# Moving five sixths of layer 1's conditioning from the attention into the scan, and keeping the sample states in a ring of six

## The reference

```python
def ada_modulation(c, w, b):
    mod = jax.nn.silu(c) @ w + b
    return jnp.split(mod[:, None, :], 6, axis=-1)
...
def modulate(h, shift, scale):
    return h * (1.0 + scale) + shift
...
    for layer in range(DEPTH):
        mp = ada_modulation(c_prompt, ada_w[layer], ada_b[layer])
        ms = ada_modulation(c_sample, ada_w[layer], ada_b[layer])
```

```python
    states = jnp.einsum('bclgn,bclgrp->bcgrpn', br, xdt * to_end[..., None])
    chunk_decay = jnp.exp(a_cum[:, :, -1])
    def step(h, inp):
        s_c, d_c = inp
        return h * d_c[..., None, None] + s_c, h
...
    y_off = jnp.einsum('bclgn,bcgrpn->bclgrp', cr, h_prev) * jnp.exp(a_cum)[..., None]
    y = (y_diag + y_off).reshape(bsz, length, nh, hp)
```

## Time and profile before

| | |
|---|---|
| median of 3 runs (lowest, highest) | 1770.33 us (1770.12, 1774.13) |
| the profiled execution, its span | 1765.11 us, 1763.3 us |
| TensorE products, weight loads | 1453.4 us (82%), 1060.0 us (60%) |
| VectorE, ScalarE, GpSimd | 651.5 us (37%), 461.8 us (26%), 210.8 us (12%) |
| mean granted clock of TensorE | 0.901 of full |
| moved by DMA | 399.72 MB, 227 GB/s over the span |
| 40 loads of `ada_w` in the attention | 1024 KB each, median 6.3 us from issue to landing |

### The profile page before, as it was taken

How to read it: one execution, slowest core, us unless ns; L and a number is a source line. 1 busy time by engine, 2 the same in 40 slices (tenths; PEclk the granted TensorE clock), 3 DMA queues, 4 the chain that set the end, 5 groups by cost and what they waited for, 6 DMA issues and landing times. The chain is left out here.

```text
span 1763.3 us, 25117 instructions
## 1 busy us (share of the span) xinstructions
PE 1453.4 (82%) x10159; PEld 1060.0 (60%) x10159; DVE 651.5 (37%) x1268; ACT 461.8 (26%) x804; POOL 210.8 (12%) x334
## 2 busy tenths in 40 slices
PE   4999789868879687799579978847999839997883
PEld 1999544446669443499345544437999826554443
DVE  3322266552336466752521111144246361111114
ACT  3212265542224352331301100032224230110012
POOL 0000033210000044100011111040000001111104
PEclk8999899879989788799779999967999969999995
DMA  7222497629932510511789999951232298999984
GB/s 294 72 90 79 184 361 265 246 108 371 364 97 72 201 46 0 203 48 49 314 327 392 384 393 397 398 182 40 81 96 76 72 411 326 385 387 396 398 303 158
DMA packets 133592, 399.72 MB, mean 227 GB/s; under 512 B 15842, under 2 KB 67682, under 8 KB 110690
## 3 DMA queue, kind: packets, MB, share of 16 engines
q1 hardware_dynamic: 114370, 359.01, 54.2%
q10 hardware_dynamic: 11488, 21.24, 3.3%
q0 software_dynamic: 7616, 17.84, 3.2%
HBM read 368.72 MB, written 37.19 MB: 230 GB/s over the span
## 5 line engine op out<-in xcount | busy, mean ns | idle before, releaser
L2889 PE MATMUL ex_gups<-ex_gu,ex_he 128*64 128x256 f32 x1728 | 211.2, 400 | 47.5 <-DMA ex_gu<-in_moe_w_up 44.6
L2889 PEld LDWEIGHTS ex_gups<-ex_gu,ex_he 128*64 128x64 f32 x1728 | 126.6, 143 | 116.0 <-DMA ex_gu<-in_moe_w_up 49.2
L2934 DVE TENSOR_TENSOR ex_hid<-ex_sg,ex_gups 128x128 f32<-128x128 f32 x64 | 18.4, 288 | 298.1 <-ACT ex_sg L2958 298.1
L2907 PE MATMUL ex_yps<-ex_dn,ex_hid_t 128*64 128x512 f32 x512 | 123.9, 604 | 0.9 <-issue 0.9
L2867 POOL DMA_INDIRECT ex_hg<-h_rows,route_tok x64 | 60.2, 941 | 508.4 <-PE ex_trps L2879 424.9
L225 PE MATMUL sc_ps<-h_hi,sc_hi 128*128 128x272 f32 x352 | 101.7, 289 | 0.5 <-PEq L3133 0.5
L225 PE MATMUL sc_ps<-hT_r,sc_hi 128*128 128x272 f32 x352 | 100.9, 287 | 0.0
L225 PE MATMUL sc_ps<-h_hi,sc_w_r 128*128 128x272 f32 x352 | 100.7, 286 | 0.0
L2958 ACT ACTIVATE ex_sg<-ex_gups 128x128 f32<-128x128 f32 x64 | 17.8, 278 | 299.2 <-PE ex_gups L2889 299.2
L2948 ACT ACTIVATE ex_yo<-ex_yps 128x512 f32<-128x512 f32 x64 | 38.3, 598 | 184.8 <-PE ex_yps L2907 184.8
L2927 DVE COPY ex_he<-ex_trps 128x512 f32<-128x512 f32 x64 | 44.3, 692 | 64.7 <-PE ex_trps L2879 64.7
(11 more groups left out here) (539 smaller groups left out, 3369.0 us busy)
## 6 DMA issues: line engine op xcount, KB each, us to landing
ex_dn<-in_moe_w_down SPq DMA_DIRECT2D x64, 1024.0 KB, 26.3
ex_gu<-in_moe_w_gate SPq DMA_DIRECT2D x54, 1024.0 KB, 24.5
ex_gu<-in_moe_w_up SPq DMA_DIRECT2D x54, 1024.0 KB, 26.5
ada_rest_w<-in_ada_w SPq DMA_DIRECT2D x40, 1024.0 KB, 6.3
as_pages<-in_cache_kT SPq DMA_DIRECT2D x32, 512.0 KB, 6.8
as_pages<-in_cache_v SPq DMA_DIRECT2D x32, 512.0 KB, 5.6
y_rows<-ex_yo ACTq DMA_DIRECT2D x128, 128.0 KB, 7.0
qkv_w<-in_mix_w_in SPq DMA_DIRECT2D x12, 1024.0 KB, 5.3
```

The lines of the kernel that those rows point to most:

```text
L2889: last = nc.tensor.matmul(gu_ps[64 * q:64 * q + 64, :, :], he[n % 2][:, j, :], ex.gu[n % S][:, :, j, q * P:(q + 1) * P], start=(j == 0), s ...
L2907: last = nc.tensor.matmul(y_ps[n % 2][64 * c:64 * c + 64, :], hid_t[:, m * CAP:(m + 1) * CAP], ex.dn[n % S][:, m, c * 512:(c + 1) * 512], ...
L2934: nc.vector.tensor_tensor(hid[:, :], sg[:, :], gu_ps[:, 1, :], ALU.mult).then_inc(done["hid"], 1)
```

## The change

- A part is 1024 columns wide. The attention makes five such parts, the last four sixths of layer 0 and the first sixth of layer 1 (20 MB, six slots). Layer 0's first two sixths are still made at the start.
- The other five sixths of layer 1 (20 MB, 40 tiles of 512 KB) are made in the scan, with two slots. Each scan step has three points on TensorE: after the decay sums, after the outputs, and at the step's end. From point 6 on (step 2) each point has one contraction tile; after eight comes a point with the part's turn (two transposes). ScalarE copies the sums, VectorE stores them at the same points, and folds the gains in step 17.
- The sample states live in a ring of six. States 6 and 7 are loaded in step 13, after states 0 and 1 have been updated and stored. Their sums are made in step 14 (before 10) and turned in step 16 (before 12); the third pair's turn stays in step 12.
- SyncE's list is written by points: the late tiles' loads, the stores of the states (each now after its own update, no longer behind the last chunk state), the wait for the first two stores.
- Chunk 3 is prepared in steps 8 to 11 (before 9 to 12).
- The conditioning takes a PSUM bank. To free it, the sums made at the start share a bank with the outputs, and the product of B and C goes into the second half of the turning bank: the next turn waits until VectorE has masked it.
- The wait for the last states' stores is also put at ScalarE's end in the next stage.

```diff
 class AdaWeights:
-    COLS = 2048
-
-    def __init__(self, k, name, parts, slots, ctx, at=None):
-        self.k, self.parts, self.slots = k, parts, slots
-        if at is None:
+    def __init__(self, k, name, parts, slots, ctx, at=None, cols=2048, rows_at=None):
+        self.k, self.parts, self.slots, self.COLS = k, parts, slots, cols
+        if rows_at is not None:
...
     def turn(self, turn_ps):
-        for c in range(4):
+        for c in range(self.COLS // 512):
...
     PREPARE = {0: [(1, 0)], 1: [(1, 1)], 2: [(1, 2)], 3: [(1, 3)],
-               4: [(2, 0)], 5: [(2, 1), (4, 0)], 6: [(2, 2), (4, 1)], 7: [(2, 3), (4, 2), (4, 3)],
-               9: [(3, 0)], 10: [(3, 1)], 11: [(3, 2)], 12: [(3, 3)]}
-    SUMS_AT, TURN_SUMS_AT = {9: (0, 1), 10: (2, 3)}, {11: (0, 1), 12: (2, 3)}
+               4: [(2, 0)], 5: [(2, 1), (4, 0)], 6: [(4, 1), (2, 2)], 7: [(2, 3), (4, 2), (4, 3)],
+               8: [(3, 0)], 9: [(3, 1)], 10: [(3, 2)], 11: [(3, 3)]}
+    SUMS_AT, TURN_SUMS_AT = {9: (0, 1), 10: (2,), 14: (3,)}, {11: (0, 1), 12: (2,), 16: (3,)}
     FIRST_UPDATE = 11
+    RING = 6
+    LATE_PARTS, LATE_SPAN, LATE_FROM = 5, KT + 1, 6
+    late_products, late_turn, late_copy = {}, {}, {}
+    for part in range(LATE_PARTS):
+        base = LATE_FROM + LATE_SPAN * part
+        for j in range(KT):
+            late_products[base + j] = (part, j)
+        late_copy[base + KT - 1], late_turn[base + KT] = part, part
...
-        sst = k.sb("sst", [P, NB, D], ctx=ctx)
-        ac_ps = k.ps("ss_acps", [P, 512], ctx)
+        sst_ring = k.sb("sst", [P, RING, D], ctx=ctx)
+        ada = AdaWeights(k, "ada_late", [(1, part) for part in range(1, 1 + LATE_PARTS)], 2, ctx, cols=1024,
+                         rows_at=k.offset["neg_ones"])
...
+        ac_ps = y_ps[1]
+        ada_bank = k.ps("ss_ada", [P, 512], ctx)
+        ada_ps = ada_bank[:, 0:256]
...
+                def load_late(m):
+                    sp.wait_ge(ada.used, m - ada.slots + 1)
+                    ada.load(sp, m // KT, m % KT)
...
+                for point in range(3 * (FIRST_UPDATE + NB)):
+                    part, j = late_products.get(point, (LATE_PARTS, 0))
+                    if part * KT + j + ada.slots < LATE_PARTS * KT:
+                        load_late(part * KT + j + ada.slots)
+                    step = point // 3
+                    if point % 3 == 1:
+                        if step == 17:
+                            sp.wait_ge(s["y"], N)
+                            out_ahead.load(sp)
+                        if step == FIRST_UPDATE + 2:
+                            sp.wait_ge(s["first_out"], 32)
+                            load_states(3)
+                    if point % 3 < 2:
+                        continue
+                    if step == POS[3, 1]:
+                        store_prompt_state()
+                    if step >= FIRST_UPDATE:
+                        store_state(step - FIRST_UPDATE)
...
                     if turn_no[c, part]:
                         pe.wait_ge(s["trc"], turn_no[c, part])
+                    if pairs_before[c, part]:
+                        pe.wait_ge(s["cbc"], pairs_before[c, part])
...
+                def condition(point):
+                    if point in late_products:
+                        part, j = late_products[point]
+                        m = part * KT + j
+                        if j == 0 and part:
+                            pe.wait_ge(ada.out, part)
+                        pe.wait_ge(ada.ready[m % ada.slots], 16 * (m // ada.slots + 1))
+                        ada.products(ada_ps, part, j)
+                    if point in late_turn:
+                        pe.wait_ge(ada.copied, late_turn[point] + 1)
+                        ada.turn(ada_ps)
...
                 for i in range(FIRST_UPDATE + NB):
                     if i < N:
                         decay_sums(i)
+                    condition(3 * i)
                     if 1 <= i <= N:
                         outputs(i - 1)
+                    condition(3 * i + 1)
...
                     if i >= FIRST_UPDATE:
                         update_product(i - FIRST_UPDATE)
+                    condition(3 * i + 2)
...
-                    rest = [(0, 1), (0, 2), (1, 0), (1, 1), (1, 2)]
-                    phase_attention_prompt(k, vtok, mixT, qn, kn, AdaWeights(k, "ada_rest", rest, 3, cw))
+                    rest = [(0, 2), (0, 3), (0, 4), (0, 5), (1, 0)]
+                    phase_attention_prompt(k, vtok, mixT, qn, kn, AdaWeights(k, "ada_rest", rest, 6, cw, cols=1024))
```

More of the change, by code:

```diff
@@ L885, in _ @@
                         dve.wait_ge(ada.turned, store_at[step] + 1)
[L886 removed]
+                        ada.store(ada_ps, store_at[step])
                     if step < STEPS:
@@ L1478, in phase_ssd, with takes @@
             if part < 3:
-                turn_no[c, part] = len(turn_no)
+                turn_no[c, part], pairs_before[c, part] = len(turn_no), pairs
+            if part == 2:
+                pairs += 1
         for t in TURN_SUMS_AT.get(step, ()):
-            turn_no["sums", t] = len(turn_no)
+            turn_no["sums", t], pairs_before["sums", t] = len(turn_no), pairs
     cb_no = {c: i for i, c in enumerate((0, 1, 2, 4, 3))}
[L1484 to L1489, removed]
+    bank_no, uses = {}, [0, 0]
+    def takes(g, *what):
+        bank_no[what] = uses[g]
+        uses[g] += 1
+    for step in range(FIRST_UPDATE + NB):
+        for t in SUMS_AT.get(step, ()):
+            takes(t % 2, "sums", t)
+        for g in range(2):
+            if step < N and UNITS[step][1] == 1:
+                takes(g, "chunk", UNITS[step][0], g)
+            if step >= FIRST_UPDATE:
+                takes(g, "update", step - FIRST_UPDATE, g)
+    names = ("made", "tr", "trc", "dA", "ac_mm", "aexp", "own_d", "xdt", "xw", "cbc", "mat", "mat4", "sums",
              "e", "decx", "m", "cs", "y", "yo", "sload", "stored", "bm", "skip4", "decayed", "oc", "masked", "own_p",
-             "zeroed", "turned", "upper")
+             "zeroed", "turned", "upper", "first_out")
     s = {n: k.sem("ss_" + n) for n in names}
@@ L1551, in _, with load_states @@
             def _(sp):
-                sp.dma_start(sst[:, :, :], io["ssm_state"]).then_inc(s["sload"], 16)
+                def load_states(t):
+                    one = (2 * t) % RING
+                    sp.dma_start(sst_ring[:, one:one + 2, :], io["ssm_state"][:, 2 * t:2 * t + 2, :]).then_inc(s["sload"], 16)
+                for m in range(ada.slots):
+                    ada.load(sp, 0, m)
+                for t in range(RING // 2):
+                    load_states(t)
                 sp.wait_ge(s["zeroed"], 1)
@@ L1556, in _, with store_state @@
                                  zeros[:, :].unsqueeze(1).to_broadcast([P, 4, 256])).then_inc(s["stored"], 16)
[L1557 to L1560, removed]
+                def load_late(m):
+                    sp.wait_ge(ada.used, m - ada.slots + 1)
+                    ada.load(sp, m // KT, m % KT)
+                def store_state(b):
@@ L1561, in _ @@
                     for g in range(2):
[L1562 to L1568 removed]
+                        sp.wait_ge(emptied[g], bank_no["update", b, g] + 1)
@@ new lines, in store_state, with store_prompt_state @@
+                    done = out_ahead.late if b >= NB - out_ahead.KEPT else s["first_out"] if b < 2 else s["stored"]
+                    sp.dma_start(io["ssm_s"][:, b, :], state(b)).then_inc(done, 16)
+                def store_prompt_state():
+                    for g in range(2):
+                        sp.wait_ge(emptied[g], bank_no["chunk", 3, g] + 1)
+                    sp.dma_start(io["ssm_p"], st[:, 1, :]).then_inc(s["stored"], 16)
+                for point in range(3 * (FIRST_UPDATE + NB)):
[14 more added lines that the diff above has]
+                        store_prompt_state()
+                    if step >= FIRST_UPDATE:
+                        store_state(step - FIRST_UPDATE)
```

91 lines of the change are left out of this document (56 added, 35 removed).

## The result

The changed kernel takes 1783.74 us in the median of five runs (1781.48 to 1788.5), the kernel before, run beside it, 1770.33 (1768.8 to 1774.13). The ratio is 1.0079, 95% interval 1.0059 to 1.0099: slower by 0.8%, 13.4 us. The forecast was 1773 with a range of 1757 to 1788, its own range 1766 to 1780; the time lies in the first, outside the second, and close to that of rival 1 (1782).

The account below looks back on a forecast made before the run. Loads were taken to bound the attention's start, TensorE most of its rest, and TensorE's work and waits for VectorE the scan. Attention -19 and scan +22 give +3 on 1770.33: 1773, own range 1766 to 1780, wider 1757 to 1788.

Parts of the forecast that it names:

- rival 1: Scan steps 2 to 9: late-tile loads decide, at 4.5 us each adding 9 us, total 1782; chance 0.26.
- The attention, -19: Attention stage: half-width products and loads make it 19 us shorter, bounds -13 and -24.
- the first term: Attention's start: the 9.0 us in which conditioning products wait for their tiles are gained.
- 13 less 3: Attention's later 28 steps: earlier score starts gain 13 us, three more half-clock spells cost 3.
- The scan, +22: Scan: 13.5 for steps 2 to 7, 6 from step 8 on, 2.5 for half clock; bounds +8 and +34.
- The steps' walk: Scan, step by step: steps 2 to 7 sum to 42.4 us, step 8 to the last update 86.2.
- The loop, steps 2 to 7: Scan: two slots, loads at 3.7 us, two products per 4.4 us; steps total 42.4 us, +13.5.
- Step 8: Scan: its first product waits about 3.4 us for the bank, the step takes 10.5 us, before 5.8.
- Step 10: Scan: this step was walked at 9.8 us.
- Steps 13 to 18: Scan's end: walked at 6.4, 11.7, 6.3, 6.9 and twice 4.9 us; late states cost step 14 about 2.5.
- Rival 2: Scan: products fill existing waits, clock stays whole, scan near +9, total 1760; chance 0.28.
- Rival 3: Attention: held by its ScalarE and VectorE chain, only 4 us go beside the DMA waits, total 1779; chance 0.08.

Follow-up runs that it names:

- Experiment 10: Kernel before, with the attention's conditioning two steps later and key and value stores held until sixteen tiles are asked for: 1764.70 us, ratio 0.9968.
- experiment 11: Kernel before, conditioning from attention step 2, one to three products per step by slack, key and value stores from the 24th tile: 1773.18 us, ratio 1.0023.
- experiment 1: Changed attention with the scan of the kernel before, layer 0's values copied for layer 1's five missing sixths: 1745.65 us, ratio 0.9868.
- experiment 3: Changed kernel loading only the first two late tiles, later products reusing them: 1936.21 us, not comparable; with layer 0's values copied in at the end 1765.59.
- Experiment 8: Changed kernel with VectorE's scaling of chunk 3 moved to the end of scan step 10: 1778.00 us, ratio 1.0047.
- Experiments 6 and 7: Two separate edits of the changed kernel: zero stores one a step in steps 8 to 15, 1785.36 us; stores of states 2 to 7 one step later, 1786.33.

## Why the prediction was right in one part and wrong in the other

**The attention, -19: right.** The stage shrank by 19.8 (bounds -13 and -24), its fourth scores start 8.3 earlier for the 9.0 taken, and the remainder gives 11.5 for the 10 that 13 less 3 make, at a clock of 0.90 for 0.92. Experiment 10 supports the first term (6.2 by later products and stores); no run splits the remainder. Wrong in detail was that no product would wait for a tile: two do, 3.6 in total. The first wait can't go, since nothing else is to be done after step 0's scores; the words left it out while the walk (first tile at about 3.8 us, measured 4.0) had it in.

**The scan, +22: mis-sized.** The profiles show +41.9, outside the bound of +34. Against the medians it is less: 13.4 + 19.8 = +33, if all else is equal. Of the 10 us between the two, 1.3 lie outside the two stages, and before's step 10 (10.4 there and in experiment 11, 13.1 in experiments 1 and 10, all with the same code) shows some 3; where the rest lies stays open. So the time fell into the range because the range was wide, not because the scan was understood: its own term was 11 to 20 too small.

The steps' walk, held against the trace: steps 2 to 7 took 10.3, 9.8, 6.9, 8.3, 7.1 and 6.8, together 49.2 for 42.4 said; step 8 9.2 for 10.5; steps 9 to 18 8.3, 14.5, 14.0, 9.3, 10.8, 12.7, 9.5 and, for the last three, 13.3, together 92.4 for 75.7. Of the 20 us by which the scan exceeds the +22, steps 13 to 18 have 10.1, step 10 4.7, steps 2 to 7 4.3 (6.8 less the 2.5 that were priced apart), the others together 0.6. **The parts that failed are the unpriced waits and half clock behind loads, and chunk 3's scaling taken as covered.**

- *The loop, steps 2 to 7.* Place and kind were right: waits of 8.9 us, steps 4 to 7 within 1.2 us each. Too small were the first two. The load for product 2, asked for at 600.84 as walked, took 6.8 and not 5 behind the zero stores, and half clock was priced once, at 2.5, where it came behind two waits, about 6 us of work each time. Without loads (experiment 3) these steps take 35.3. A load took 4.3 in the median for 3.7. The Trainium skill, "DMA: Bandwidth & Descriptors", on the anatomy of one DMA, gives 3.2 as an estimate by its fixed 2.0 us and 436 GB/s, for the GpSimd path; of the 40 loads that SyncE issued here the quickest took 3.6, so for them the measurement decides.
- *Step 8, 9.2 for 10.5.* Right: GpSimd's product no longer slows the chunk's scaling (1.21 for 4.39). Wrong: it doesn't slow the samples' scaling either (1.21, begun 0.1 before it), and the 3.4 us of waiting at step 8's first product never came.
- *Steps 11 and 12*, 14.0 and 9.3 for 13.0 and 9.2 said: right, one turn of the sums went from step 12, and step 11's turn waits 2.7 for the mask.
- *Step 10, 14.5 for 9.8: wrong.* The walk moved chunk 3's scaling here and priced it as cover, beside TensorE's work. But it is ahead of the sample sums. Beside GpSimd's two products, VectorE's decay product took 2.43, the scaling 2.59 and the state's decay behind it 1.21. The slowing is not the move's: in before the state's decay itself took 2.59 at this place. What the move adds is one more product, and VectorE turned to the sums 6.5 us after the decay product's start, for 3.7 in before and 5.4 in experiment 1. Experiment 8 shows its worth: 4 to 6 us in the median.
- *Steps 13 to 18, 46.3 for 36.2.* The walk had no wait for a tile there. There are two, 1.96 and 1.27, when stores of states stand between the loads, and each has a spell at half clock behind it (an update 3.77 for 1.98, a decay product 1.67 for 1.02). Without loads these steps take 39.5, so 6.8 of the 10.1 come from the loads. Experiments 6 and 7 moved stores without gain, so that the stores are the cause is not shown. Step 14's late states were seen (12.7 for 11.7).
- *Clock.* Said was a higher granted clock in the scan; it was 0.83 for 0.84. With no load to wait for it is 0.88, with three slots 0.91. The Trainium skill, "TensorE: Matmul & The Clock Gate", under what is actually happening, has throttled as the default that activity releases. The traces agree in so far as the clock was half behind the waits (0.50 after 4.88 us of standing); but more products raised its mean only where they brought few waits or none.

**The rivals.** Rival 1's time came (1782), and mostly its place (14 of the loads' 23 us in the profiles fall in steps 2 to 7). Its mechanism holds in part: it reckoned 9 us for loads of 4.5 in place of 3.7, and by that the median of 4.3 makes 7. But the depth weighs more: a third slot takes 10 to 12 us of the loads' 18 to 20 away though tiles land later. Rival 2 failed by its condition, that the added products bring no new waits. Without loads the whole is faster than before (-5.7 us), but not its 1760. Rival 3 failed: the attention gave more than 4 beyond the waits.

**What each part costs**, by ratios: attention -23 (by its stage -20), the rearrangement +4 (within the intervals nothing, by its stage nothing), products and turns +14, loads +18 to +20. They add up by construction to the 12 to 14 us measured. Since step 10's order costs 4 to 6 in the full kernel and stands in the rearrangement, these parts aren't independent. Three slots and the later scaling together were not tried.

## What to carry to other kernels

Before moving work into a stage because its DMA engines are idle, work out the loop from freeing a slot over the load to the product against the distance of two uses: two slots at three uses a step cost here more than the products themselves, and one slot more took over half of it back. Busy time that moves need not be absorbed (here 7 us of 24 were), and an operation moved one step earlier must be priced against everything queued behind it on its engine. If a stage waits for loads only at its start, try first to use them later (experiment 10: 5.7 us) before moving the work out of it; packed closer, the same loads bound more steps (experiment 11).

## What the runs showed of the hardware

- A wait of TensorE is paid again in clock: after 4.88 us of standing the next products took 1.08 and 2.08 for 0.64 and 1.02, for 5.7 us, and again for about 6 us after 2.82. Experiment 8 took 3.1 us from one wait, and step 10 became 5.0 shorter.
- A 512 KB load asked for alone landed in 3.8 us, with two on their way in 4.3, with three slots in 4.8 (medians); behind 4 MB of stores it took 6.8.
- VectorE and GpSimd slowed each other, and with starts 0.02 us apart or less either could be the one that paid. In step 10 VectorE's 128x512 product took 0.68 and GpSimd's two 128x1024 products 5.29, or 2.44 and 4.21: both outcomes came with the same code (0.68 in before and experiment 11, 2.44 in experiments 1 and 10). With the order clear it was the later one: the 128x1024 scaling begun 0.3 us after GpSimd's 32x2048 took 4.39 for 1.21, GpSimd's 3.59; beside a 32x1024 scaling begun 0.1 before it (1.21) GpSimd's took 4.58. No run was made for this alone.
- The scan with the code of before took 117.0, 121.1, 121.5 and 115.4 us in four executions (before, experiments 1, 10 and 11), so the length of a stage read from one profile is uncertain by some 3 us each way.
